# A hybrid GLA and Hyena layer: half-size transforms of the long convolution, longer strips before the second norm, and moved accumulations

## The reference, cut to what matters

```python
def long_conv_bidir(u, h_fwd, h_bwd, skip):      # u (B, L=256, 1024)
    k_full = concatenate([h_fwd, zeros, h_bwd[:0:-1]])
    k_f = rfft(k_full); u_f = rfft(u, n=2 * L)
    y = irfft(u_f * k_f, n=2 * L)[:, :L]
    return y + u * skip

z = h @ w_in                                     # q k v lr g zh mg
la = log_sigmoid(lr @ wg + bg) / 16              # decays of the GLA
o = gla(q, k, v, la_f, s0_f) + flip(gla(flip(q), flip(k), flip(v), flip(la_b), s0_b))
o = rmsnorm(o) * silu(g)
x0, x1, v = split(short_conv3(zh)); y_hy = long_conv_bidir(v * x1, h_fwd, h_bwd, skip) * x0
mix = (sigmoid(gate_a) * (o @ p_gla) + sigmoid(gate_b) * (y_hy @ p_hy)) @ w_out
x1 = x + gate * rmsnorm(mix) * n_post_mix
out = x1 + gate2 * rmsnorm(swiglu(modulate(rmsnorm(x1)))) * n_post_ffn
```

## Time and profile before

| | us |
|---|---|
| median of 3 runs | 1647.66 |
| lowest, highest | 1646.72, 1648.83 |
| the profiled execution | 1644.38 |
| its span, first to last instruction | 1642.6 |
| TensorE busy in it | 1605.4 |
| VectorE busy | 1087.7 |
| ScalarE busy | 747.7 |
| DMA moved | 378.26 MB, 230 GB/s |
| mean granted clock of TensorE | 0.995 |

### The profile page before, as it was taken

One profiled execution on the slowest core, in us unless ns is written; L12 is line 12 of the kernel. 1 busy time (PEld: TensorE's weight loads), 2 busy tenths in 40 slices (PEclk: granted clock), 3 DMA queues, 4 the chain that ended last, 5 costly groups with the idle time before them and its releaser, 6 DMA issues.

```text
span 1642.6 us, 22553 instructions
## 1 busy us (share of the span) xinstructions
PE 1605.4 (98%) x8556; PEld 1312.7 (80%) x8556; DVE 1087.7 (66%) x1296; ACT 747.7 (46%) x899; POOL 80.0 (5%) x155
## 2 busy tenths in 40 slices
PE   6899999999999999999998999999999999999998
PEld 4466677888888888888887888888888888888886
DVE  3667787678778658778876666666666555555556
ACT  5432326643543334444445555554455544444444
POOL 0011020000000000100010000000000000000000
PEclk9999999999999999999998999999999999999999
DMA  9989968666566768977795677777776566566553
GB/s 330 334 295 331 326 209 282 190 203 188 175 213 205 238 194 267 285 229 229 265 325 180 205 240 233 232 240 232 235 238 202 190 186 200 191 192 193 192 193 125
DMA packets 264497, 378.26 MB, mean 230 GB/s; under 512 B 14145, under 2 KB 223404, under 8 KB 262764
## 3 DMA queue, kind: packets, MB, share of 16 engines
q1 hardware_dynamic: 243008, 297.57, 57.1%
q0 software_dynamic: 20528, 79.43, 14.2%
q10 hardware_dynamic: 892, 0.33, 0.1%
HBM read 373.09 MB, written 4.19 MB: 230 GB/s over the span
## 4 chain that ended last, share of the span: by engine, by line
PE 92%; DVE 3%; DMA 3%; issue 1%; ACT 0%; ACTq 0%; SPq 0%; DVEq 0%
PE ps L1610 39%; PE ps L1616 19%; PE ps L1624 8%; PE ps L1626 8%; PE ps L1625 8%; PE ps L1550 1%; DMA a2k<-in_w_ada 1%; PE ps L1540 1%; PE ps L1787 1%; PE ps L1779 1%; DMA ada_raw<-in_w_ada 1%; DVE acck L1024 1%; DVE lo L1092 1%; PE ps L1748 1%; PE ps L1760 0%
## 5 line engine op out<-in xcount | busy, mean ns | idle before, releaser
L1092 DVE TENSOR_TENSOR lo<-raw,hi 128x1024 fp32r<-128x1024 f32 x480 | 583.0, 1222 | 329.5 <-ACT hi L855 247.5
L1610 PE MATMUL ps<-hx,hi 128*128 128x512 f32 x1408 | 443.9, 397 | 2.1 <-DVE hx L1380 1.3
L855 ACT ACTIVATE hi<-raw 128x1024 fp32r<-128x1024 f32 x252 | 266.8, 1060 | 317.0 <-PE ps L1616 203.9
L605 ACT ACTIVATE hi<-raw 128x1024 fp32r<-128x1024 f32 x228 | 241.0, 1060 | 296.9 <-PE ps L1616 180.2
L1610 PE MATMUL ps<-hxc,hi 128*128 128x512 f32 x1088 | 346.8, 400 | 0.0
L1616 PEld LDWEIGHTS ps<-hx,lo 128*128 128x128 f32 x1408 | 264.8, 188 | 62.6
L1616 PE MATMUL ps<-hx,lo 128*128 128x256 f32 x1408 | 276.9, 278 | 0.0
L1616 PEld LDWEIGHTS ps<-hxc,lo 128*128 128x128 f32 x1088 | 204.4, 188 | 48.2
L1610 PEld LDWEIGHTS ps<-hx,hi 128*128 128x128 f32 x1408 | 214.8, 189 | 3.9 <-issue 1.6
L1616 PE MATMUL ps<-hxc,lo 128*128 128x256 f32 x1088 | 213.9, 278 | 0.0
L1610 PEld LDWEIGHTS ps<-hxc,hi 128*128 128x128 f32 x1088 | 166.4, 189 | 9.3 <-issue 7.1
(11 more groups left out here) (300 smaller groups left out, 1618.4 us busy)
## 6 DMA issues: line engine op xcount, KB each, us to landing
raw<-in_w_in SPq DMA_DIRECT2D x160, 512.0 KB, 4.5
a2raw<-in_w_ada POOLq DMA_DIRECT2D x96, 512.0 KB, 5.3
raw<-in_ffn_gate SPq DMA_DIRECT2D x88, 512.0 KB, 4.6
raw<-in_ffn_up SPq DMA_DIRECT2D x88, 512.0 KB, 4.5
raw<-in_ffn_down SPq DMA_DIRECT2D x88, 512.0 KB, 4.5
ada_raw<-in_w_ada SPq DMA_DIRECT2D x64, 512.0 KB, 9.6
a2k<-in_w_ada POOLq DMA_DIRECT2D x32, 512.0 KB, 6.2
raw<-in_w_out SPq DMA_DIRECT2D x32, 512.0 KB, 5.1
```

What stands on the lines that cost most here:

```text
L605: nc.scalar.activation(hi[:, uu % 4, :], raw[:, slot_of(uu), :], ACT.Copy).then_inc(hi_done, 1)
L855: nc.scalar.activation(hi[:, slot, :], raw[:, uu % RING, :], ACT.Copy).then_inc(hi_done, 1)
L1092: V.tensor_tensor(lo[:, slot_of(uu), :], raw[:, slot_of(uu), :], hi[:, uu % 4, :].bitcast(f32), SUB).then_inc(lo_done, 1)
L1610: mm(bank(b + t), hi[:, uu % 4, c0:c0 + P], feat[:, k, :], start=first, stop=False)
```

## The change

1. *Transforms by even and odd positions.* With the frequencies at half-odd places, frequency k and its partner 255 - k have the same products up to signs: the transform of the even positions A and of the odd positions B (128 frequencies each) give A + B and A - B (up to conjugation). So `fwd` holds 128 frequencies for the 128 even and the 128 odd positions, half as large; `uturn`, the filters and their window are ordered by even and odd; `spectrum` and `dft` use one product where there were two. The steps are now, for each half of the channels, `ksum` (sum and difference of the filter spectra, VectorE), `dft` (8 records x 1 on TensorE for both A and B, a ScalarE copy of B to `ab`, sums and differences on VectorE), `prod_a`, `prod_b` (6 VectorE instructions each) and `gsum` (4). `idft` has 16 products of 128 columns a step, and its evacuation reads PSUM in even and odd order. All later steps move by 3 or 4 units.
2. *Strips.* `NW = 6` units of `w_out` in strips instead of 3; the high halves of the last two of them and of the first two FFN units go to a buffer of their own, `hi_w`.
3. *Norm.* The gain, the square sum and the scaling of token tile 0 move ahead of the end of the `w_out` products; the cuts of FFN unit 1 too; 14 small products (`keep_running(14)`) follow the column sums.
4. *Schedules.* Modulation products of block 1 stand behind pieces 2, 4, 6 and 8, its fifth moves into block 2, its columns behind piece 9; `A2_AT` is changed from accumulation 51 on.

```diff
@@ STEPS and tables
-        STEPS += [("dft", i, 90 + 5 * i, "pd") for i in range(4)]
-        STEPS += [("idft", 0, 113, "pd"), ("idft", 1, 117, "pd"), ("red", 0, 124, "pd"),
-                  ("cut", 0, 127, "d"), ("row", 0, 130, "d"), ("cut", 1, 136, "d")]
+        for i in range(2):
+            STEPS += [("ksum", i, 88 + 14 * i, "d"), ("dft", i, 91 + 14 * i, "pad"),
+                      ("prod_a", i, 94 + 14 * i, "d"), ("prod_b", i, 97 + 14 * i, "d"),
+                      ("gsum", i, 100 + 14 * i, "d")]
+        STEPS += [("idft", 0, 117, "pd"), ("idft", 1, 121, "pd"), ("red", 0, 127, "pd"),
+                  ("cut", 0, 130, "d"), ("row", 0, 133, "d"), ("cut", 1, 139, "d")]
...
-        A2_AT = ([28 + int(2.4 * a) for a in range(19)] + [99 + 2 * a for a in range(13)]
-                 + [134 + 2 * a for a in range(13)] + [160 + 6 * a for a in range(5)]
+        A2_AT = ([28 + int(2.4 * a) for a in range(19)] + [81, 86, 91, 96, 99, 102, 105, 108, 110, 112, 119, 121, 123]
+                 + [138 + int(1.7 * a) for a in range(13)] + [160 + 6 * a for a in range(5)]
...
-                 {0: "a", 1: "a", 3: "a", 5: "a", 7: "tc", 10: "a"}]
-        AFTER += [{0: "a", 1: "t", 3: "a", 5: "a", 7: "c", 10: "a"} for _ in range(NB - 4)]
+                 {2: "a", 4: "a", 6: "a", 8: "a", 9: "tc"},
+                 {0: "a", 1: "at", 3: "a", 5: "a", 7: "c", 10: "a"}]
+        AFTER += [{0: "a", 1: "t", 3: "a", 5: "a", 7: "c", 10: "a"} for _ in range(NB - 5)]
-        MOD_AT = 7
+        MOD_AT = [0, 9] + [7] * (NB - 2)
...
-            pool.wait_ge(x_sem["d"], upto(STEPS, "d", stepno("dft", 3)))
+            pool.wait_ge(x_sem["d"], upto(STEPS, "d", stepno("gsum", 1)))
@@ ScalarE, the second norm
             cut_high(NM)
+            cut_high(NM + 1)
...
             quarter(1, 1024, 15).then_inc(w_sq, 1)
+            act.wait_ge(j_x, 1)
+            link(x_square(0, 0, D, 22))
+            root(24, 22, eps[:, 0:1]).then_inc(j_act, 1)
             act.wait_ge(mm_done, NM)
@@ VectorE, the steps
+                    for ri in range(2):
+                        ins = V.tensor_tensor(ab[:, 0, ri], bank(ri), ab[:, 1, ri], ADD)
+                    link(ins)
+                    for ri in range(2):
+                        ins = V.tensor_tensor(ab[:, 1, ri], bank(ri), ab[:, 1, ri], SUB)
+                    ins.then_inc(done, 1)
...
+                elif name in ("prod_a", "prod_b"):
+                    V.tensor_tensor(tf[:, 0], ab[:, n_, 0], kr, MUL)
+                    V.tensor_tensor(tf[:, 1], ab[:, n_, 1], ki, MUL)
+                    V.tensor_tensor(tf[:, 2], ab[:, n_, 0], ki, MUL)
+                    link(V.tensor_tensor(tf[:, 3], ab[:, n_, 1], kr, MUL))
                     V.tensor_tensor(kr, tf[:, 0], tf[:, 1], SUB)
                     V.tensor_tensor(ki, tf[:, 2], tf[:, 3], ADD).then_inc(done, 1)
@@ VectorE, the second norm
             gain(0, 0, 1024)
+            gain(0, 1024, D).then_inc(j_x, 1)
...
             gated_quarter(1024)
-            gain(0, 1024, D).then_inc(j_x, 1)
+            unit_low(NM + 1)
+            dve.wait_ge(j_act, 2)
+            link(V.reciprocal(st[:, 26:27], st[:, 24:25]))
+            scaled(0, 0).then_inc(f_dve, 1)
+            scaled(0, 1)
@@ TensorE
-                for t in range(2):
-                    ins = mm(bank(7), fwd[:, t, 256 * k + P * i:256 * k + P * (i + 1)],
-                             src[:, t, 512 * half:512 * (half + 1)], start=(t == 0), stop=(t == 1))
+                ins = mm(bank(7), fwd[:, i, k, :], src[:, i, 512 * half:512 * (half + 1)], start=True,
+                         stop=True)
...
-                    f, half = i // 2, i % 2
-                    for ri in range(2):
-                        for t in range(2):
-                            ins = mm(bank(ri), fwd[:, t, 256 * ri + P * f:256 * ri + P * (f + 1)],
-                                     ut[:, t, 512 * half:512 * (half + 1)], start=(t == 0),
-                                     stop=(t == 1))
+                    for e in range(2):
+                        for ri in range(2):
+                            ins = mm(bank(2 * e + ri), fwd[:, e, ri, :],
+                                     ut[:, e, 512 * i:512 * (i + 1)], start=True, stop=True)
...
-                        for m in range(4):
-                            ins = mm(ps[:, 256 * k:256 * (k + 1)],
-                                     kk2[:, m % 2, m // 2, P * ch:P * (ch + 1)], inv[:, m, :],
-                                     start=(m == 0), stop=(m == 3))
+                        for e in range(2):
+                            for ri in range(2):
+                                ins = mm(ps[:, 256 * k + P * e:256 * k + P * (e + 1)],
+                                         kk2[:, e, ri, P * ch:P * (ch + 1)],
+                                         inv[:, ri, P * e:P * (e + 1)], start=(ri == 0),
+                                         stop=(ri == 1))
...
             column_sums().then_inc(j_cols, 1)
+            keep_running(14)
```

More of the change, by code:

```diff
@@ L29 @@
 K_ID, K_ONE, K_TRI, K_TRC, K_REL, K_FWD = 0, 128, 256, 640, 896, 1408
-K_SEL = K_FWD + 1024
+K_SEL = K_FWD + 512
 K_END = K_SEL + 32
@@ L308, in enter_step, with high_of @@
                     eng.wait_ge(sems[e], v)
+        NW = 6
+        IN_HI_W = [NM - 2, NM - 1, NM, NM + 1]
+        def high_of(uu):
+            return hi_w[:, IN_HI_W.index(uu), :] if uu in IN_HI_W else hi[:, uu % 4, :]
         RESULTS = [(0, 0, 1024), (0, 1024, D), (1, 0, 1024), (1, 1024, 1536), (1, 1536, D)]
@@ L353, in nth_unit @@
         def nth_unit(b, idx):
-            return 4 * (b + 1) + (b > 1) + sum(AFTER[b].get(i, "").count("a") for i in range(idx))
+            return 4 + sum(what.count("a") for b_ in range(b + 1) for i, what in AFTER[b_].items()
+                           if b_ < b or i < idx)
         def piece(b, idx):
@@ L1288, in step @@
                     V.tensor_tensor(kr, tf[:, 0], tf[:, 1], SUB)
                     V.tensor_tensor(ki, tf[:, 2], tf[:, 3], ADD).then_inc(done, 1)
+                elif name == "gsum":
+                    dve.wait_ge(done, upto(STEPS, "d", n - 1))
+                    half = slice(512 * i, 512 * (i + 1))
+                    for ri in range(2):
+                        ins = V.tensor_tensor(kk2[:, 1, ri, half], kk2[:, 0, ri, half], kb[:, ri], SUB)
+                    link(ins)
+                    for ri in range(2):
+                        ins = V.tensor_tensor(kk2[:, 0, ri, half], kk2[:, 0, ri, half], kb[:, ri], ADD)
+                    ins.then_inc(done, 1)
@@ L1604, in rank_products, with high_products @@
                 return ins
-            def high_products(b, uu, kq, feat, k, first):
+            def high_products(b, uu, kq, feat, k, first, w_h=None):
                 for t in range(2):
                     c0 = 256 * kq + P * t
-                    mm(bank(b + t), hi[:, uu % 4, c0:c0 + P], feat[:, k, :], start=first, stop=False)
+                    mm(bank(b + t), (hi[:, uu % 4, :] if w_h is None else w_h)[:, c0:c0 + P],
+                       feat[:, k, :], start=first, stop=False)
             def low_products(b, uu, kq, feat, k, last):
@@ L1840, in _ @@
                         spectrum(SPEC_AFTER[idx])
-            for uu in range(NKV, NM - 3):
+            for uu in range(NKV, NM - NW):
                 unit(uu)
@@ L1845, in _ @@
                         step(n)
-            for uu in range(NM - 3, NM):
+            for uu in range(NM - NW, NM):
                 pe.wait_ge(lo_done, uu + 1)
@@ L1875, in ffn_unit @@
                         pe.wait_ge(n_dve, 2 * q + kq // 2 + 1)
-                    high_products(4 * k + 2 * up, NM + j, kq, hx2, 4 * q + kq, q == kq == 0)
+                    high_products(4 * k + 2 * up, NM + j, kq, hx2, 4 * q + kq, q == kq == 0,
+                                  high_of(NM + j) if first else None)
                     ins = low_products(4 * k + 2 * up, NM + j, kq, hx2, 4 * q + kq,
@@ L1893, in _ @@
                 if j in (5, 9, 13):
-                    ffn_unit(j // 4 - 1)
+                    ffn_unit(j // 4 - 1, first=True)
             for j in range(3, 8):
```

86 lines of the change are left out of this document (51 added, 35 removed).

## The result

The changed kernel takes 1635.35 us (median of 4, 1633.33 to 1637.49) against 1647.20 us (median of 4) for the kernel before on the same chip: 0.9929 of its time, 95% interval 0.9917 to 0.9940. The prediction was 1633, range 1621 to 1642. The profiled execution took 1634.57 us, span 1632.8; the one of the kernel before 1644.38.

The account below looks back on a forecast made before the run. TensorE was taken as the bound; -2.5 - 6.3 - 6.9 - 5.5 + 7.3 + 0.5 - 0.6 = -14.0 us gave 1630.4 from the profiled execution, 1633.7 from the median; forecast 1633, range 1621 to 1642.

Parts of the forecast that it names:

- The frame: Whole kernel: TensorE, busy 98%, is the bound; its removed products count at full price unless VectorE or the DMA becomes late.
- Spectra, `dft`: k/v phase and forward transforms: halved products save 6.3 us (3 to 6.9) on spectra and 6.9 us on `dft`.
- `idft`: Inverse transforms: records of 128 columns at 0.13 us each save 5.5 us, bounds 5.1 and 6.9.
- The stall: Unit 81: VectorE waits for load 51, delaying unit 83; 7.3 us lost, bounds 1.2 and 9.
- no slack at all: Units 81 to 83: VectorE has no slack, so the accumulation instruction alone costs at least 1.2 us.
- Strides and the interleaved evacuation: Transposes of `u` and inverse evacuation: strides taken as 0; doubling would be 1.75 us, and 3.8 us of VectorE.
- VectorE in the transform stretch: Units 91 to 101: 34.9 us of VectorE work against TensorE's 31.4 just fits; +0.5 us, bounds 0 and 3.
- the rival on VectorE: Units 88 to 117: VectorE becomes the bound and the kernel slower; 1656 us at 1.2 us an instruction, chance 0.05.
- Block 1: k/v phase: reordered modulation units remove 6.0 us of waits, part returns; 2.5 us saved, bounds 0 and 6.
- The rest of the k/v phase: k/v phase from 183 us, and the decays: change forecast as 0, with no term in the sum.
- early savings are eaten: Block 1 refills with waits and loads behind 130 us come late: 7 us taken back, 1640 us, chance 0.20.
- The turn: `w_out` to FFN: earlier norm work, but 14 products partly at half clock; 0.6 us saved, bounds -3 and +2.

Follow-up runs that it names:

- experiment 1: Changed kernel with accumulations 51 and 52 at units 86 and 88: 1626.48 us; or with their loads issued earlier, accumulation 51 still at unit 81: 1627.49 us.
- Experiment 3: Changed kernel with the 13 second-chunk accumulations back at every second unit from 99, as in the kernel before: 1625.33 us, 0.9868.
- the direct experiment: Changed kernel with the old order of block 1 of the k/v phase: 1635.67 us, 0.9933.
- e2: Changed kernel with loads 51 and 52 issued ahead of the wait for the last mix and the filter-spectra reload: 1627.49 us, 0.9882.
- e4: Changed kernel with 7 keep-running products in the turn instead of 14: 1630.86 us, 0.9907.
- e11: Changed kernel with the 13 second-chunk accumulations at every second unit from 99, where the kernel before has them: 1625.33 us, 0.9868.
- e1: Changed kernel with accumulations 51 and 52 moved from units 81 and 86 to units 86 and 88: 1626.48 us, 0.9877.
- e3: Changed kernel without the 14 keep-running products behind the column sums of the turn: 1633.14 us, 0.9915.
- experiment 5: Changed kernel with the old order of block 1: 1635.67 us, 0.9933; its table compares block 1's length and clock across traces.
- e7: Kernel before with the change's transforms alone, and the accumulations after the second chunk from unit 138 instead of 134: 1631.41 us, 0.9908.
- e6: Kernel before with accumulation 51 alone moved from unit 99 to unit 81: 1655.92 us, 1.0054.
- experiment 8, e9: Combined kernel (e8) with one first-chunk modulation accumulation moved from ahead of columns(7) to behind it: 1626.40 us, 0.9884.
- e5: Changed kernel with the old order of block 1 (modulation units behind pieces 0, 1, 3, 5, 10; columns(2) behind piece 7): 1635.67 us, 0.9933.
- e10: Kernel before with the change's turn to the FFN alone (six strip units, new norm order, 14 products): 1644.69 us, 0.9987.
- e8: Changed kernel, accumulations 51 and 52 at units 86 and 88, no 14 products, block 1 filter products behind pieces 1, 4, 6, 8: 1623.22 us, 0.9859.

## Why the prediction was right, and where it was not

**The frame held.** That TensorE's products come off at full price, and that something late would have to give part back, is what the traces show. The time is 2.4 us above the forecast, inside the range. Part of the closeness is luck: in the traces the saving is 4.2 us short of the forecast (9.8 for 14.0), with terms off both ways, and the medians lie 2.1 us further apart than the two traces.

**Spectra, `dft`.** 7.0 for 6.3 and 6.9 for 6.9. The safety margin on the spectra was not needed at that place, but see below.

**`idft`.** The mechanism was right and the size off: 0.112 us for a record of 128 columns and not 0.13, so 6.7 us saved instead of 5.5. I had taken the row of `cp,toks` (0.128 each), which is a step of 12 short transposes with its start and end in it; the end of the bound from streaming alone, 0.108, was the nearer.

**The stall.** The step is confirmed from four sides: take the wait away by place or by an earlier load, -8.9 and -7.9 us; put it into the kernel before, +8.8; the trace, 7.2 against 7.3 forecast, with 5.87 us of waiting against "6 to 7". That the trace meets the forecast to a tenth is luck, since four traces of the same code have 7.2 to 8.6 us; the 0.9 us for half clock was the small part. Only "no slack at all", and the lower bound of 1.2 us with it, rested on a misreading (experiment 1).

**Strides and the interleaved evacuation.** The strided transposes cost 0.18 us for 16. The evacuation of the inverse transform, median between least and most of its 8 instructions in ns:

```profile
L1344 DVE SCALAR_TENSOR_TENSOR yhy<-u,col,ps x8: 474/477/481, 576.2 to 589.1; 128x256 f32<-128x256 f32 x8
```

The group of the kernel before had 476: reading PSUM in the interleaved order, 256 fp32 values per partition with 512 bytes from one to the next in turn, costs nothing here. The Trainium skill (SBUF — State Buffer, section "Door 1: The DMA port swizzle") says that a non-contiguous pattern in PSUM slows matmuls significantly; it does not speak of reads by VectorE, and for this one the measurement shows no slowdown. Of SBUF the same section says that reads which hit each 16-byte line at least twice run at full bandwidth, as a stride of two fp32 values does; the trace is near it, but 10% longer (1.93 against 1.75 us).

**VectorE in the transform stretch.** 0.2 for 0.5. The count (34.9 us of work against 31.4 and a lead of 3 to 6) was good enough, and the mean of 0.69 us an instruction held. (In the rival on VectorE, 30 x 2.80 + 6.9 is 90.9 us and not 90.6; nothing changes by it.) Experiment 3 adds that even the old, dense list fits, with less cover at load 61.

**Block 1: the step that failed.** I counted 6.0 us of waits gone, 3.6 back and 2.5 saved. The trace has 0.5 with the start-up and 1.0 without it, and the direct experiment cannot tell the term from nothing. The count of waits was not what failed: where the clock stays up (e2, e4) the new order saves 2.2 to 2.6 us, though with a wait of 0.97 us more than I had listed, for ScalarE's features in front of filter product 0, and one of 0.8 us in the old order that I had not listed either. What failed is that the clock stood in the sum at nothing. Behind the waits of 1.0 and 2.4 us it fell in four of six traces, and that took back about 1.5 us of the 2.5 (3.0 in e11). The changed kernel's stretch 64 to 72 us:

```profile
64.00:68.00 4.00, 2.97 (x10) 1.84 (x11) 3.80 (x7) 0.00 (x0) 0.00 (x0) 0.84 1.07 364
68.00:72.00 4.00, 4.00 (x18) 2.25 (x18) 2.74 (x5) 1.06 (x1) 0.00 (x0) 0.74 1.09 362
```

and the same in e2, where it stays up:

```profile
64.00:68.00 4.00, 1.95 (x8) 1.07 (x9) 3.76 (x8) 0.00 (x0) 0.00 (x0) 1.00 1.06 368
68.00:72.00 4.00, 4.00 (x22) 1.90 (x20) 3.51 (x6) 0.94 (x1) 0.00 (x0) 1.00 1.09 363
```

The same code, and the products of the changed kernel stood 0.43 us apart from 67 to 70 us and not 0.23. e1, e3 and e11 show the fall too, e2 and e4 do not (the table in experiment 5 has the distances).

**The rest of the k/v phase: the line that was not in the sum.** The rival "early savings are eaten" had it at 0.20, with 7 us, at "loads behind 130 us". It happened at 3 us, and later than I had put it: up to 176 us nothing is lost, and then 3.1 us in the changed kernel, 4.0 in e2, 3.4 in e7. Since e6 lost the same 3.1 us with the long spectra, only about 1.7 us of it, the difference of the averages, can be put down to the change. In the changed kernel TensorE waits 0.65 us for `hxc` at 215 us, and the clock falls at 230.5:

```profile
228.00:232.00 4.00, 3.88 (x22) 3.49 (x23) 1.18 (x2) 0.27 (x1) 0.11 (x1) 0.82 0.26 91
232.00:236.00 4.00, 4.00 (x15) 3.19 (x14) 3.18 (x6) 0.79 (x1) 0.00 (x0) 0.76 0.48 131
```

In e2 it does not fall there, and 3.3 us are waits instead: 2.0 for `hxc`, the others for `modc`, `vc` and `lr`, each under 0.7. So the loss is not one stall but a chain of small ones, and they stand where VectorE waits for `a2k`, longer in e6 (4.1 us) than in the kernel before (2.6). That these loads are its cause is argued from the waits and was not shown: experiment 8 moved the loss, and did not take it away. This stays open.

**The turn.** -0.6 forecast; +0.4 in the traces, about -2 (0.7 to 3.6) by the run of it alone. I had the 14 products at "some 5 us together, until 892.9" and they took 5.4, so their half clock was right; the rows were ready some 2.7 us before their end, where I had forecast 1.3 (891.6 against 892.9).

**The parts as measured** leave 3.2 us open: transforms -15.2, turn -2.1, block 1 -0.3, stall +8.9 make -8.7, and the whole made -11.9 by medians. The 2.2 us at load 61, which the transforms alone lost and the changed kernel did not, would be most of it; that is argued and not shown, since each of these terms is known to 1 or 2 us only.

## What to carry to other kernels

Before an instruction moves to an earlier place, look up when its data is issued and landed, not how long the instruction takes: here one list entry cost more than five times the instruction's own 1.28 us, and issuing the load earlier made the same place free. When work comes off a bound engine in a phase whose other engines wait for loads, ask what is late next and count the gain only up to there. A filler that keeps an engine busy must be counted at the clock it will really get, and end when the next work is ready; that it should is read from the traces here, and no median settles it. And a term of 1 to 3 us is read from more than one trace, between two marks close around it, with the clock of each trace beside it: the same block saved 2.5 us or 1 by whether the clock fell.

## What the runs showed of the hardware that I had not expected

- **The granted clock falls in some executions of the same code and not in others.** Behind filter product 1 (65 to 72 us) it fell in the changed kernel, e1, e3 and e11, not in e2 and e4, which run the same instructions up to there; with the old order of block 1 it fell at 60 to 64 us in e5, e6 and e7, not in the kernel before and e10. Behind the shift sums (some 231 to 235 us) it fell in the changed kernel, e5, e6 (there at 238) and e11, not in e2, e3, e4, e7, e8, e10 and the kernel before; in e1 it fell at 218 us and in e9 at 224. Most of these falls lasted 3.4 us, and such a fall made block 1 in its new order 1.5 us longer; the one of 6.8 us in e11 made it 3.0 longer. So one trace against another tells an effect of 1 to 2 us in these places only after the clock of both has been read.
- **The column sums of the turn** (32 records of one column) took 3.5 to 4.7 us, as the clock fell behind or inside them.
- **Landing times of one and the same load differ**: 6.3 and 8.9 us for load 61, issued at the same place; 9.1 in the changed kernel.
- **fp32 products of 128 columns** stand 0.112 us apart when 32 records follow one another, 0.216 for 256 columns: by these two, a fixed part is under 0.01 us a record.
